# Two pairs of gathered rows per unit on TensorE, through the same two buffers, in units 1 to 7 of a PEER layer

## The chip, the cores and the metric

One core of one Trainium2 chip. The metric is the device time of one execution in microseconds (us); lower is better.

## The reference, cut to what matters

One decoder layer over 256 tokens of width 2048. Its last part is a PEER feed-forward: for each token and each of 8 heads, two searches of the best 16 of 128 keys give 16 experts out of 16,384, and then

```python
u = peer_u[eb]                                   # (256 tokens, 128 chosen rows, 2048)
a = gelu(einsum('td,tkd->tk', xb, u))            # one dot product per token and row
out = einsum('tk,tkd->td', wb * a, peer_v[eb])
```

The change is about the first einsum: 256 x 128 rows of `peer_u` have to be gathered, and each is dotted with its token's `h1`.

## The kernel before, in words

The 128 partitions hold 128 tokens. A **unit** is one head of one half of the tokens: units 0 to 7 are the first half (T = 0), 8 to 15 the second. A unit has 16 rows, k = 0 to 15; row k is one gather (`gather_u`, L1833): one indirect DMA issued by GpSimd (POOL) that fetches, for each of the 128 tokens, one row of 2048 floats, 1 MB in all. POOL issues all gathers in a written order, each behind the wait for its buffer (`wait_free`, L1819).

There are eight buffers of 1 MB. Six form a ring for the rows dotted on VectorE (DVE): the gather of such a row waits until the dot of the row six places earlier is done. Two more hold rows 0 and 1 of a unit, the **pair**. DVE's dot is one instruction (L1633) of 128x2048 with both inputs in SBUF. The pair goes another way (`dots_pair`, L814): in 8 blocks, TensorE (PE) turns two 128-column pieces of both rows into PSUM (L826), ScalarE (ACT) copies the block to `ut` (`pair_copies`, L1204), and PE multiplies it with `h1` turned (`products`, L830). Two buffers each for the PSUM block and `ut` carry it from engine to engine. At the end, `pair_dots` (L1637) on DVE picks the diagonal of the product, two instructions of 128x128 with one input in PSUM. The two buffers of the pair are free as soon as the eighth block is turned (semaphore `ut_turned`), before the products end.

Unit 0 uses DVE only. In units 1 to 15 DVE does 9 dots (k = 2 to 10), the pair's two short instructions, and 5 dots (k = 11 to 15). In units 1 to 13 the steps of the search for the unit after next (`topk`, L1569) stand between them. POOL gathers k = 0 to 15 in order, the pair first; in unit 1 four ring rows come before the pair. After unit 15 the second einsum starts: gathers of `v_rows` for part of the columns, and dense panels of `peer_v` on PE for the others.

Of the kernel before, what the change touches and what calls it, by code (L numbers as in the profile page):

```python
# [33 lines left out]
PH, NKEY, TOPK = 8, 128, 16  # L34
# [32 lines left out]
RING = 8  # L67
HEAD_RING = 4

PAIR = (0, 1)  # L70
PAIR_AFTER = 9
ROW_RING = 6
BLOCKS = KT // 2
PER_UNIT = P // 4 // 8
# [41 lines left out]
def decoder_layer(nc, x, meta_tokens, ln0_g, ln0_b, w_in, b_if, conv_w, mh_norm_w, p_a, p_b, w_o,  # L116
# [5 lines left out]
    with ctx:  # L122
# [155 lines left out]
        def S(name):  # L278
            if name not in sems:
                sems[name] = ctx.enter_context(nc.semaphore(name))  # L280
            return sems[name]
# [23 lines left out]
        u_in = [S(f"u_in{j}") for j in range(RING)]  # L305
# [5 lines left out]
        TOKR = [(0, META), (META, P), (META + P, P)]  # L311
        HCRED, BCRED = SLOT_N, NB

        def dot_place(u, k):

            if u == 0:
                return k + 1
            if k in PAIR:
                return u * TOPK + PAIR_AFTER + k + 1
            return u * TOPK + k - 1 + (2 if k - 2 >= PAIR_AFTER else 0)  # L320

        def row_number(u, k):

            return (u - 1) * (TOPK - 2) + k - 2

        def row_slot(u, k):
            if u == 0:
                return k % HEAD_RING
            return ROW_RING + k if k in PAIR else row_number(u, k) % ROW_RING

        def wait_row(eng, u, k):

            j = row_slot(u, k)
            if u == 0:
                eng.wait_ge(u_in[j], 16 * (k // HEAD_RING + 1))
            elif k in PAIR:
                eng.wait_ge(u_in[j], 16 * u)
            else:
                eng.wait_ge(u_in[j], 16 * ((TOPK // HEAD_RING if j < HEAD_RING else 0) + row_number(u, k) // ROW_RING + 1))

# [13 lines left out]
        def _(sp):  # L354
# [57 lines left out]
            for i in range(NKEY):  # L412
                j = i % RAWS
                if i == 0:
                    sp.wait_ge(S("topk_done"), NT * PH)
                elif i == 1:
                    sp.wait_ge(S("ut_used"), (2 * PH - 1) * BLOCKS)
                elif i == 3:
                    sp.wait_ge(S("dots_done"), 2 * PH * TOPK)
                elif i >= RAWS:  # L420
                    sp.wait_ge(S("panel_done"), i - RAWS + 1)
                set_apart(sp)
                sp.dma_start(v_raw[j][:, :], peer_v[i * P:(i + 1) * P, :]).then_inc(vr_in[j], 16)
                if i == NKEY - 8:

                    sp.wait_ge(S("panel_done"), 64)
                    for t, v in ((g2_bc, ln2_g), (b2_bc, ln2_b)):
                        sp.dma_start(t[:, :], v[0].partition_broadcast(P)).then_inc(S("bc2_in"), 16)
# [8 lines left out]
        def _(pe):  # L437
# [241 lines left out]
            for g in range(3):  # L679
                tokens_group(g + G_WO, mh, ml, 0, g % 2, wo_free(g),  # L680
                             {1: lambda: sum_blocks(3), 6: lambda: residual(0)} if g == 0 else {2: lambda: residual(g)},
                             before=merged_wait if g == 0 else None)
# [128 lines left out]
                    last = mm(ps[:, 3 * T + n, 0:b - a], alpha_i[:, :], h1[:, T, a:b], True, False)  # L811
                last.then_inc(S("tile_opened"), 1)

            def dots_pair(u):  # L814

                T, m = u // PH, u - 1
                o = ps[:, 5 - 3 * (m % 2), 0:256]

                def turn(b):
                    g = m * BLOCKS + b  # L820
                    if g >= 2:
                        pe.wait_ge(S("ut_copied"), g - 1)
                    for n in range(2):
                        for r, k in enumerate(PAIR):
                            kt = 2 * b + n
                            last = nc.tensor.transpose(ps[:, 3 + g % 2, (2 * n + r) * P:(2 * n + r + 1) * P],  # L826
                                                       u_rows[row_slot(u, k)][:, kt * P:(kt + 1) * P], ident[:, :])
                    last.then_inc(S("ut_turned"), 1)

                def products(b):  # L830
                    g = m * BLOCKS + b
                    pe.wait_ge(S("ut_copied"), g + 1)
                    if b == 0 and m >= 2:
                        pe.wait_ge(S("dots_done"), dot_place(u - 2, PAIR[1]))
                    for n in range(2):
                        kt = 2 * b + n
                        last = mm(o, h1t[T][:, kt, :], ut[:, g % 2, n * 256:(n + 1) * 256], kt == 0, kt == KT - 1)
                    last.then_inc(S("ut_used"), 1)

                for k in PAIR:  # L840
                    wait_row(pe, u, k)
                turn(0)
                for b in range(BLOCKS):
                    if b + 1 < BLOCKS:
                        turn(b + 1)
                    products(b)
# [29 lines left out]
            h1_turn(0)  # L876
            h1_turn(1)
            for u in range(1, 2 * PH):
                dots_pair(u)
                if u == PH:  # L880
                    slots_turn(0)
                if u >= PH:
                    for c in range((u - PH) * PER_UNIT, (u - PH + 1) * PER_UNIT):
                        place(c)
# [22 lines left out]
        def _(act):  # L907
# [293 lines left out]
                    A(h1t[T][:, 4 * c:4 * c + 4, :].rearrange("p a t -> p (a t)"), ps[:, bank, :], ACT.Copy  # L1201
                      ).then_inc(S("h1t_copied"), 1)

            def pair_copies(u):  # L1204
                for b in range(BLOCKS):
                    g = (u - 1) * BLOCKS + b
                    act.wait_ge(S("ut_turned"), g + 1)
                    if g >= 2:
                        act.wait_ge(S("ut_used"), g - 1)
                    A(ut[:, g % 2, :], ps[:, 3 + g % 2, :], ACT.Copy).then_inc(S("ut_copied"), 1)  # L1210
# [50 lines left out]
            gelu(0)  # L1261
            softmax_exp(2)
            for u in range(1, 2 * PH):
                pair_copies(u)
                if u > 1:
                    gelu(u - 1)
                if 3 <= u + 1 < 2 * PH:
                    softmax_exp(u + 1)
                if u == PH:
                    slots_copy(0)  # L1270
                    act.wait_ge(S("slots_copied"), 1)
                if u >= PH:
                    for c in range((u - PH) * PER_UNIT, (u - PH + 1) * PER_UNIT):
                        one_hots(c)
                        if c % PER_UNIT:
                            w_copy(c - 1)
                    w_copy(c)
# [10 lines left out]
        def _(dve):  # L1288
# [345 lines left out]
                                       h1[:, u // PH, :], ALU.mult, ALU.mult,  # L1634
                                       accum_out=dots[:, u % 2, k:k + 1]).then_inc(S("dots_done"), 1)

            def pair_dots(u):  # L1637

                m = u - 1
                dve.wait_ge(S("ut_used"), (m + 1) * BLOCKS)  # L1640
                for r, k in enumerate(PAIR):
                    bank = 5 - 3 * (m % 2)
                    dve.wait_ge(S("dots_done"), dot_place(u, k) - 1)
                    V.scalar_tensor_tensor(junk2[:, :], ps[:, bank, r * P:(r + 1) * P], 1.0, ident[:, :], ALU.mult, ALU.mult,
                                           accum_out=dots[:, u % 2, k:k + 1]).then_inc(S("dots_done"), 1)
# [51 lines left out]
            dve.wait_ge(S("sc_copied"), NT * 4)  # L1697
            topk(2, scores_of(2), {6: lambda: coefs(0)})

            def unit_part(u, n):  # L1700

                if n == PAIR_AFTER:
                    pair_dots(u)
                else:
                    dot(u, n + 2 if n < PAIR_AFTER else n + 1)
                if n == 8 and u > 1:
                    coefs(u - 1)
                if n == 8 and u == PH:
                    scale_acc(0)

            for u in range(1, 2 * PH):
                parts = TOPK - 1
                if u + 2 < 2 * PH:
                    topk(u + 2, scores_of(u + 2), {n + 1: lambda n=n: unit_part(u, n) for n in range(parts)})
                else:
                    for n in range(parts):
                        unit_part(u, n)
# [44 lines left out]
        def _(pool):  # L1762
# [56 lines left out]
            def wait_free(u, k):  # L1819

                if u == 0:
                    if k >= HEAD_RING:
                        pool.wait_ge(S("dots_done"), dot_place(0, k - HEAD_RING))
                elif k in PAIR:
                    if u > 1:
                        pool.wait_ge(S("ut_turned"), (u - 1) * BLOCKS)
                elif row_number(u, k) >= ROW_RING:
                    before = row_number(u, k) - ROW_RING
                    pool.wait_ge(S("dots_done"), dot_place(before // (TOPK - 2) + 1, before % (TOPK - 2) + 2))
                elif row_slot(u, k) < HEAD_RING:  # L1830
                    pool.wait_ge(S("dots_done"), dot_place(0, TOPK - HEAD_RING + row_slot(u, k)))

# [23 lines left out]
            for k in range(TOPK):  # L1856
                gather_u(0, k)
            indices(1)
            for k in range(2, 2 + HEAD_RING):
                gather_u(1, k)  # L1860
            pool.wait_ge(S("halves_used"), GROUPS * HALVES + HCRED)
            pool.wait_ge(S("qk_done"), NT * 4)
            for k in PAIR + tuple(range(2 + HEAD_RING, TOPK)):
                gather_u(1, k)
            for u in range(2, 2 * PH):
                indices(u)
                for k in range(TOPK):
                    gather_u(u, k)
            for n in range(NT * SLOTS):
                gather_v(n)  # L1870
# [33 lines left out]
```

## Time and profile before

| | |
|---|---|
| median of 3 runs | 2397.64 us (2397.33 to 2400.06) |
| the profiled execution, its own time | 2398.14 us |
| span of that execution, first to last instruction | 2396.3 us |
| mean granted TensorE clock | 0.904 of full speed |
| gathers of rows of u: first and last of units 1 to 15 | about 1221 us to 1805 us |

The span has three parts: dense projections, bound by PE, to about 1240 us; the dots, to about 1845 us; the second einsum, to the end. POOL's records need care: one lasts from when the engine takes the gather up to when its descriptors are written, and it can be stretched by a wait inside it. The DMA share is that of 16 queues; it passes 1 slightly because packets overlap.

### The profile page before, as it was taken

Reading aid. Unit: us, or ns where it says so; the run is one execution under the profiler, and the core shown is the slowest. Engines: PE = TensorE matmul, PEld = TensorE weight load, DVE = VectorE, ACT = ScalarE, POOL = GpSimd, SP = SyncE. Lnnn points to the kernel's source line nnn. Section 1 sums busy time; section 2 is a strip of 40 time slices with the busy share of each in tenths; the row PEclk is TensorE's granted clock in tenths of the full one; section 3 lists DMA queues with packets and bytes.
Section 4 is the critical chain, followed back from the end, with each engine's and each line's share of the span. In section 5 each row is a group of like instructions: output and inputs, shape, how many; then the busy total and the mean of one; then the engine's idle time right before and its main releaser. Section 6 shows DMA issues by size and latency. Waiting matters only on the chain.

```text
span 2396.3 us, 30725 instructions
## 1 busy us (share of the span) xinstructions
PE 1975.6 (82%) x10800; PEld 1619.9 (68%) x10800; DVE 1603.7 (67%) x2299; ACT 868.5 (36%) x1467; POOL 952.2 (40%) x559
## 2 busy tenths in 40 slices
PE   6999999999999999999972424264645899999996
PEld 5888899998888988887961313253534666666663
DVE  5444455455444555555989999999997866666666
ACT  4444434444444444446431212278685500000000
POOL 0000000000000000000248888888885288878884
PEclk9999999999999999999996756566656999999998
DMA  5444465655655655552989999999998299999997
GB/s 164 127 139 139 141 191 168 200 177 180 194 188 176 202 184 189 189 181 91 366 335 399 420 421 421 409 420 418 411 419 343 106 411 412 411 410 411 411 407 286
DMA packets 217056, 675.01 MB, mean 282 GB/s; under 512 B 18784, under 2 KB 68320, under 8 KB 183520
## 3 DMA queue, kind: packets, MB, share of 16 engines
q0 software_dynamic: 57488, 393.25, 40.3%
q1 hardware_dynamic: 159456, 280.32, 35.3%
q8 instruction: 64, 1.05, 0.2%
q14 instruction: 48, 0.39, 0.0%
HBM read 671.42 MB, written 2.10 MB: 281 GB/s over the span
## 4 chain that ended last, share of the span: by engine, by line
PE 47%; issue 22%; POOL 10%; DMA 10%; DVE 9%; ACT 2%; DVEq 0%; POOLq 0%; ACTq 0%; SPq 0%
PE ps L439 46%; DMA u_rows<-in_peer_u,idx_all 8%; POOL v_rows L1851 7%; POOL u_rows L1838 3%; DMA v_rows<-in_v_gathered,idx_all 2%; DVE junk L1633 2%; DVE ohs L1666 1%; ACT hi L911 0%; DVE ohs L1663 0%; DVE h L1681 0%; PE ps L524 0%; DVE st L1328 0%; DVE ki L1593 0%; DVE pos L1606 0%; DVE pos L1603 0%
## 5 line engine op out<-in xcount | busy, mean ns | idle before, releaser
L1296 DVE TENSOR_TENSOR lo<-raw,hi 128x1024 fp32r<-128x1024 f32 x368 | 448.6, 1225 | 489.5 <-ACT hi L911 488.9
L1838 POOL DMA_INDIRECT u_rows<-in_peer_u,idx_all x256 | 537.5, 2100 | 170.9 <-issue 73.6
L911 ACT ACTIVATE hi<-raw 128x1024 fp32r<-128x1024 f32 x376 | 397.3, 1059 | 568.2 <-PE ps L439 561.5
L1633 DVE SCALAR_TENSOR_TENSOR junk<-u_rows,h 128x2048 bf16<-128x2048 f32 x226 | 514.7, 2280 | 31.9 <-DMA u_rows<-in_peer_u,idx_all 31.9
L439 PE MATMUL ps<-v_raw,wt 128*128 128x368 f32 x1536 | 475.4, 472 | 2.8 <-DMA v_raw<-in_peer_v 2.0
L1851 POOL DMA_INDIRECT v_rows<-in_v_gathered,idx_all x256 | 391.8, 1530 | 147.4 <-issue 79.6
L439 PE MATMUL ps<-xh,hi 128*128 128x256 f32 (+2 forms) x1536 | 440.6, 287 | 2.4 <-ACT qkv L911 1.3
L439 PE MATMUL ps<-xh,lo 128*128 128x256 f32 (+2 forms) x1536 | 435.6, 284 | 0.0
L439 PE MATMUL ps<-xl,hi 128*128 128x256 f32 (+2 forms) x1536 | 435.0, 283 | 0.0
L1681 DVE SCALAR_TENSOR_TENSOR h<-v_rows,coef_all,h 128x944 f32<-128x944 f32 x256 | 307.6, 1202 | 173.4 <-DMA v_rows<-in_v_gathered,idx_all 172.2
L439 PEld LDWEIGHTS ps<-v_raw,wt 128*128 128x128 f32 x1536 | 291.7, 190 | 186.2 <-DMA v_raw<-in_peer_v 2.6
L1784 POOL TENSOR_TENSOR rstd<-rstd,m_half 128x1 f32<-128x1 f32 (+1 forms) x7 | 5.8, 823 | 820.1 <-DVE rstd L1537 800.4
L439 PEld LDWEIGHTS ps<-xh,hi 128*128 128x128 f32 x1536 | 290.4, 189 | 12.2 <-issue 8.5
L439 PEld LDWEIGHTS ps<-xl,hi 128*128 128x128 f32 x1536 | 290.9, 189 | 0.0
L439 PEld LDWEIGHTS ps<-xh,lo 128*128 128x128 f32 x1536 | 290.2, 189 | 0.0
L826 PE MATMUL ps<-ident,u_rows 128*128 128x128 f32 x480 | 87.2, 321 | 208.3 <-issue 196.5
L826 PEld LDWEIGHTS ps<-ident,u_rows 128*128 128x128 f32 x480 | 73.2, 170 | 223.7 <-issue 214.7
L439 PE MATMUL ps<-ohs 128*128 128x128 f32 x512 | 102.1, 363 | 136.8 <-ACT ohs L911 126.2
L439 PEld LDWEIGHTS ps<-ohs 128*128 128x128 f32 x512 | 87.8, 259 | 152.2 <-ACT ohs L911 136.4
L911 ACT ACTIVATE ut<-ps 128x512 f32<-128x512 f32 x120 | 71.6, 597 | 291.8 <-PE ps L826 291.8
L439 PE MATMUL ps<-ut,h1t 128*128 128x256 f32 x480 | 140.1, 424 | 0.1
L439 PE MATMUL ps<-hi,xh 128*128 128x512 f32 x256 | 101.8, 398 | 1.8 <-DVE t_y L1452 1.3
(227 smaller groups left out, 2497.1 us busy)
## 6 DMA issues: line engine op xcount, KB each, us to landing
raw<-in_w_in SPq DMA_DIRECT2D x96, 1024.0 KB, 5.4
v_raw<-in_peer_v SPq DMA_DIRECT2D x128, 552.0 KB, 7.8
raw<-in_w_in SPq DMA_DIRECT2D x64, 256.0 KB, 3.2
raw<-in_w_in SPq DMA_DIRECT2D x32, 512.0 KB, 4.6
raw<-in_p_a SPq DMA_DIRECT2D x16, 1024.0 KB, 5.0
raw<-in_p_b SPq DMA_DIRECT2D x16, 1024.0 KB, 5.0
raw<-in_w_o SPq DMA_DIRECT2D x16, 1024.0 KB, 5.0
raw<-in_peer_wq SPq DMA_DIRECT2D x16, 1024.0 KB, 6.8
```

The source lines that it names most:

```text
L439: return nc.tensor.matmul(o, a, b, start=start, stop=stop)
L826: last = nc.tensor.transpose(ps[:, 3 + g % 2, (2 * n + r) * P:(2 * n + r + 1) * P], u_rows[row_slot(u, k)][:, kt * P:(kt + 1) * P], ident[ ...
L911: return nc.scalar.activation(o, i, f, **kw)
L1296: V.tensor_tensor(raw_lo[:, hh // 2, k4, :] if kept else lo[:, hh % SLOT_N, :, :], raw[:, hh // 2, k4, :], (kept_hi(hh) if kept else hi[:, ...
L1633: V.scalar_tensor_tensor(junk[:, n % 2, :], u_rows[row_slot(u, k)][:, :], 1.0, h1[:, u // PH, :], ALU.mult, ALU.mult, accum_out=dots[:, u ...
L1666: ins = V.tensor_scalar(o[:, 0, q, :], iota[:, :], slots_t[:, 1, t0 + q:t0 + q + 1], slots_t[:, 0, t0 + q:t0 + q + 1], ALU.is_equal, ALU.mult)
L1681: V.scalar_tensor_tensor(h1[:, T, FD:D], v_rows[n % VRING][:, :], coef_all[:, T, s:s + 1], h1[:, T, FD:D], ALU.mult, ALU.add).then_inc(S(" ...
L1784: Q.tensor_tensor(rstd[:cnt, n:n + 1], rstd[:cnt, n:n + 1], m_half[:cnt, 0:1], ALU.pow).then_inc(S(name + "_rstd"), 1)
L1838: Q.indirect_dma_start(u_rows[slot][:, :], None, peer_u, bass.IndirectOffsetOnAxis(ap=idx_all[:, n:n + 1], axis=0)).then_inc(u_in[slot], 16)
L1851: Q.indirect_dma_start(v_rows[n % VRING][:, :], None, v_gathered, bass.IndirectOffsetOnAxis(ap=idx_all[:, n:n + 1], axis=0)).then_inc(v_in ...
```

## The change

Units 1 to 7 send two pairs through PE, rows 0 and 1 and rows 2 and 3; units 8 to 15 keep one pair. Both pairs of a unit use the same two buffers, so the second pair's gathers wait until the first pair has been turned, and the next unit's first pair until the second has. POOL's order in units 2 to 7 becomes: first pair, 6 ring rows, second pair, 6 ring rows. In unit 1: ring rows 4 to 7, first pair, rows 8 and 9, second pair, rows 10 to 15. DVE's order becomes: 9 dots, first pair's two short instructions, 3 dots, second pair's two. The sizes of all buffers stay.

```diff
-PAIR = (0, 1)
-PAIR_AFTER = 9
+PAIRS = (0,) + (2,) * (PH - 1) + (1,) * PH
+PAIR_AFTER = (9, 14)
+SECOND_GATHERED = 6
...
+        def dot_order(u):
+
+            rows, order = vector_rows(u), []
+            for n in range(TOPK):
+                for q in range(PAIRS[u]):
+                    if len(order) == PAIR_AFTER[q] and pair_rows(q)[0] not in order:
+                        order += pair_rows(q)
+                if rows:
+                    order.append(rows[0])
+                    rows = rows[1:]
+            for q in range(PAIRS[u]):
+                if pair_rows(q)[0] not in order:
+                    order += pair_rows(q)
+            return tuple(order)
...
+        def gather_order(u):
+
             if u == 0:
-                return k + 1
...
+                return tuple(range(TOPK))
+            rows = vector_rows(u)
+            order = pair_rows(0) + rows
+            if PAIRS[u] == 2:
+                order = pair_rows(0) + rows[:SECOND_GATHERED] + pair_rows(1) + rows[SECOND_GATHERED:]
+            return order
...
         def row_slot(u, k):
             if u == 0:
                 return k % HEAD_RING
-            return ROW_RING + k if k in PAIR else row_number(u, k) % ROW_RING
+            return ROW_RING + k % 2 if k < 2 * PAIRS[u] else row_number(u, k) % ROW_RING
...
             for u in range(1, 2 * PH):
-                dots_pair(u)
+                for q in range(PAIRS[u]):
+                    dots_pair(u, q)
...
             for u in range(1, 2 * PH):
-                pair_copies(u)
+                pair_copies(u, 0)
                 if u > 1:
                     gelu(u - 1)
                 if 3 <= u + 1 < 2 * PH:
                     softmax_exp(u + 1)
+                if PAIRS[u] == 2:
+                    pair_copies(u, 1)
...
-                elif k in PAIR:
-                    if u > 1:
-                        pool.wait_ge(S("ut_turned"), (u - 1) * BLOCKS)
+                elif k < 2 * PAIRS[u]:
+                    if pair_number(u, k // 2):
+                        pool.wait_ge(S("ut_turned"), pair_number(u, k // 2) * BLOCKS)
...
-            for k in PAIR + tuple(range(2 + HEAD_RING, TOPK)):
-                gather_u(1, k)
+            for k in gather_order(1):
+                if k not in vector_rows(1)[:HEAD_RING]:
+                    gather_u(1, k)
             for u in range(2, 2 * PH):
                 indices(u)
-                for k in range(TOPK):
+                for k in gather_order(u):
                     gather_u(u, k)
```

`vector_rows(u)` are the rows from 2 x PAIRS[u] to 15, `pair_number(u, q)` counts the pairs through PE, and the numbers that the semaphores are waited for follow the new orders.

## Rows read from the trace of the kernel before

**Rows 1.** The page: busy time by engine, and DMA over 40 slices of 59.9 us.

```profile
PE 1975.6 (82%) x10800; PEld 1619.9 (68%) x10800; DVE 1603.7 (67%) x2299; ACT 868.5 (36%) x1467; POOL 952.2 (40%) x559
...
DMA  5444465655655655552989999999998299999997
GB/s 164 127 139 139 141 191 168 200 177 180 194 188 176 202 184 189 189 181 91 366 335 399 420 421 421 409 420 418 411 419 343 106 411 412 411 410 411 411 407 286
```

**Rows 2.** Stretches: start:end, length, busy PE PEld DVE ACT POOL, clock, DMA share, GB/s.

```profile
1343.00:1424.00 81.00, 25.84 (x128) 21.45 (x128) 78.58 (x143) 15.92 (x26) 71.22 (x33) 0.65 1.01 421
1248.00:1250.00 2.00, 2.00 (x14) 1.72 (x13) 2.00 (x7) 1.10 (x2) 1.70 (x2) 1.00 0.55 147
```

**Rows 3.** Timeline of DVE in unit 14 (no search steps): two dots in succession.

```profile
1781.41 2.29 DVE L1633 SCALAR_TENSOR_TENSOR junk<-u_rows,h 128x2048 bf16<-128x2048 f32 x1 [0.19 <-DMA u_rows<-in_peer_u,idx_all]
...
1783.89 2.29 DVE L1633 SCALAR_TENSOR_TENSOR junk<-u_rows,h 128x2048 bf16<-128x2048 f32 x1 [0.18 <-DMA u_rows<-in_peer_u,idx_all]
```

**Rows 4.** Timeline of PE: a pair's first and last turned blocks, units 1, 2 and 8.

```profile
1242.43 1.94 PE L826 MATMUL ps<-ident,u_rows 128*128 128x128 f32 x8 [11.75 <-DMA u_rows<-in_peer_u,idx_all]
...
1252.48 0.60 PE L826 MATMUL ps<-ident,u_rows 128*128 128x128 f32 x4
...
1275.51 1.94 PE L826 MATMUL ps<-ident,u_rows 128*128 128x128 f32 x8 [20.61 <-issue]
...
1286.08 0.60 PE L826 MATMUL ps<-ident,u_rows 128*128 128x128 f32 x4
...
1519.78 1.94 PE L826 MATMUL ps<-ident,u_rows 128*128 128x128 f32 x8 [27.07 <-issue]
...
1531.08 0.60 PE L826 MATMUL ps<-ident,u_rows 128*128 128x128 f32 x4
```

**Rows 5.** Timeline of POOL: the gathers that matter in units 1 and 2.

```profile
1234.14 0.94 POOL L1838 DMA_INDIRECT u_rows<-in_peer_u,idx_all  x1 [0.30 <-issue]
1243.03 0.93 POOL L1838 DMA_INDIRECT u_rows<-in_peer_u,idx_all  x1 [7.95 <-DVE junk L1633]
...
1265.23 2.75 POOL L1838 DMA_INDIRECT u_rows<-in_peer_u,idx_all  x1 [0.30 <-DVE junk L1644]
1268.28 2.58 POOL L1838 DMA_INDIRECT u_rows<-in_peer_u,idx_all  x1 [0.30 <-issue]
1271.17 2.58 POOL L1838 DMA_INDIRECT u_rows<-in_peer_u,idx_all  x1 [0.30 <-issue]
```

**Rows 6.** Timeline of DVE in units 1 and 2: dots beside those gathers.

```profile
1239.94 2.27 DVE L1633 SCALAR_TENSOR_TENSOR junk<-u_rows,h 128x2048 bf16<-128x2048 f32 x1
...
1253.69 2.27 DVE L1633 SCALAR_TENSOR_TENSOR junk<-u_rows,h 128x2048 bf16<-128x2048 f32 x1
...
1267.77 2.28 DVE L1633 SCALAR_TENSOR_TENSOR junk<-u_rows,h 128x2048 bf16<-128x2048 f32 x1
1269.98 0.08 DVE L1633 DVE_READ_ACCUMULATOR junk<-u_rows,h 128x1 f32 x1
```

**Rows 7.** The gathers started from 1214 to 1215 us, to an idle queue: record and landing.

```profile
L1838 POOL DMA_INDIRECT u_rows<-in_peer_u,idx_all x1: 1137/1137/1137, 1214.8 to 1214.8; - x1
...
DMA to landing us min/median/max: 5.6/5.6/5.6
```

**Rows 8.** The gathers started from 1204 to 1206 us, beside a dot: record and landing.

```profile
L1838 POOL DMA_INDIRECT u_rows<-in_peer_u,idx_all x1: 2954/2954/2954, 1205.0 to 1205.0; - x1
...
DMA to landing us min/median/max: 7.5/7.5/7.5
```

**Rows 9.** Stretches around one pair's turning in unit 5 (columns as in rows 2).

```profile
1396.00:1398.00 2.00, 0.09 (x1) 0.12 (x2) 2.00 (x4) 0.00 (x0) 1.72 (x1) 0.50 1.02 426
...
1404.00:1406.00 2.00, 2.00 (x13) 1.77 (x13) 2.00 (x3) 1.16 (x2) 2.00 (x1) 1.00 1.01 422
...
1410.00:1412.00 2.00, 1.13 (x5) 0.67 (x4) 2.00 (x5) 1.97 (x3) 2.00 (x1) 1.00 1.03 430
...
1414.00:1416.00 2.00, 0.00 (x0) 0.00 (x0) 2.00 (x2) 0.00 (x0) 1.69 (x2) 0.50 1.02 426
```

More of the change, by code:

```diff
@@ L312, in decoder_layer, with vector_rows, pair_rows, pair_number @@
         HCRED, BCRED = SLOT_N, NB
+        def vector_rows(u):
+            return tuple(range(2 * PAIRS[u], TOPK))
+        def pair_rows(q):
+            return (2 * q, 2 * q + 1)
+        def pair_number(u, q):
+            return sum(PAIRS[:u]) + q
+        def dot_order(u):
[11 more added lines that the diff above has]
+            return tuple(order)
         def dot_place(u, k):
+            return u * TOPK + dot_order(u).index(k) + 1
+        def gather_order(u):
             if u == 0:
-                return k + 1
-            if k in PAIR:
-                return u * TOPK + PAIR_AFTER + k + 1
-            return u * TOPK + k - 1 + (2 if k - 2 >= PAIR_AFTER else 0)
-        def row_number(u, k):
-            return (u - 1) * (TOPK - 2) + k - 2
+                return tuple(range(TOPK))
[4 more added lines that the diff above has]
+            return order
+        def row_number(u, k):
+            return sum(len(vector_rows(w)) for w in range(1, u)) + k - 2 * PAIRS[u]
+        def row_of_number(n):
+            u = 1
+            while n >= len(vector_rows(u)):
+                n, u = n - len(vector_rows(u)), u + 1
+            return u, vector_rows(u)[n]
         def row_slot(u, k):
@@ L335, in wait_row @@
                 eng.wait_ge(u_in[j], 16 * (k // HEAD_RING + 1))
-            elif k in PAIR:
-                eng.wait_ge(u_in[j], 16 * u)
+            elif k < 2 * PAIRS[u]:
+                eng.wait_ge(u_in[j], 16 * (pair_number(u, k // 2) + 1))
             else:
@@ L416, in _ @@
                 elif i == 1:
-                    sp.wait_ge(S("ut_used"), (2 * PH - 1) * BLOCKS)
+                    sp.wait_ge(S("ut_used"), sum(PAIRS) * BLOCKS)
                 elif i == 3:
@@ L812, in tile_open, with dots_pair @@
                 last.then_inc(S("tile_opened"), 1)
-            def dots_pair(u):
-                T, m = u // PH, u - 1
+            def dots_pair(u, q):
+                T, m = u // PH, pair_number(u, q)
                 o = ps[:, 5 - 3 * (m % 2), 0:256]
@@ L823, in turn @@
                     for n in range(2):
-                        for r, k in enumerate(PAIR):
+                        for r, k in enumerate(pair_rows(q)):
                             kt = 2 * b + n
@@ L833, in products @@
                     if b == 0 and m >= 2:
-                        pe.wait_ge(S("dots_done"), dot_place(u - 2, PAIR[1]))
+                        w, z = next((w, z) for w in range(2 * PH) for z in range(PAIRS[w]) if pair_number(w, z) == m - 2)
+                        pe.wait_ge(S("dots_done"), dot_place(w, pair_rows(z)[1]))
                     for n in range(2):
@@ L838, in products @@
                     last.then_inc(S("ut_used"), 1)
-                for k in PAIR:
+                for k in pair_rows(q):
                     wait_row(pe, u, k)
@@ L1202, in h1_copy, with pair_copies @@
                       ).then_inc(S("h1t_copied"), 1)
-            def pair_copies(u):
+            def pair_copies(u, q):
                 for b in range(BLOCKS):
-                    g = (u - 1) * BLOCKS + b
+                    g = pair_number(u, q) * BLOCKS + b
                     act.wait_ge(S("ut_turned"), g + 1)
@@ L1635, in dot, with pair_dots @@
                                        accum_out=dots[:, u % 2, k:k + 1]).then_inc(S("dots_done"), 1)
-            def pair_dots(u):
-                m = u - 1
+            def pair_dots(u, q):
+                m = pair_number(u, q)
                 dve.wait_ge(S("ut_used"), (m + 1) * BLOCKS)
-                for r, k in enumerate(PAIR):
+                for r, k in enumerate(pair_rows(q)):
                     bank = 5 - 3 * (m % 2)
@@ L1698, in _, with unit_steps @@
             topk(2, scores_of(2), {6: lambda: coefs(0)})
+            def unit_steps(u):
+                order = dot_order(u)
+                return [k for k in order if k >= 2 * PAIRS[u] or k % 2 == 0]
             def unit_part(u, n):
-                if n == PAIR_AFTER:
-                    pair_dots(u)
+                k = unit_steps(u)[n]
+                if k < 2 * PAIRS[u]:
+                    pair_dots(u, k // 2)
                 else:
-                    dot(u, n + 2 if n < PAIR_AFTER else n + 1)
+                    dot(u, k)
                 if n == 8 and u > 1:
@@ L1711, in _ @@
             for u in range(1, 2 * PH):
-                parts = TOPK - 1
+                parts = len(unit_steps(u))
                 if u + 2 < 2 * PH:
@@ L1823, in wait_free @@
                         pool.wait_ge(S("dots_done"), dot_place(0, k - HEAD_RING))
-                elif k in PAIR:
-                    if u > 1:
-                        pool.wait_ge(S("ut_turned"), (u - 1) * BLOCKS)
+                elif k < 2 * PAIRS[u]:
+                    if pair_number(u, k // 2):
+                        pool.wait_ge(S("ut_turned"), pair_number(u, k // 2) * BLOCKS)
                 elif row_number(u, k) >= ROW_RING:
-                    before = row_number(u, k) - ROW_RING
-                    pool.wait_ge(S("dots_done"), dot_place(before // (TOPK - 2) + 1, before % (TOPK - 2) + 2))
+                    pool.wait_ge(S("dots_done"), dot_place(*row_of_number(row_number(u, k) - ROW_RING)))
                 elif row_slot(u, k) < HEAD_RING:
@@ L1858, in _ @@
             indices(1)
-            for k in range(2, 2 + HEAD_RING):
+            for k in vector_rows(1)[:HEAD_RING]:
                 gather_u(1, k)
```

## The prediction, made before the change was built

> **What bounds the kernel now.** I read the page first, to find the stretch that the change touches: from about 1260 us the DMA row stands at 9 and the rate at 399 to 421 GB/s until the dots end [rows 1]. Then the windows: over 81 us of it DVE is busy for 78.6, so it is nearly full as well, beside a DMA share of 1.01 at 421 GB/s [rows 2]. Which of the two sets the pace they can't say. The timeline of unit 14 settles it: there are no search steps, DVE waits before each dot for a row to land, and dots follow each other at 1783.89 - 1781.41 = 2.48 us [rows 3]. A row of 1.0486 MB in 2.49 us is 421 GB/s, the rate of the middle units as well. So sixteen rows cost at least 16 x 2.49 = 39.8 us of transfer. The real pace comes from PE's first turn in units 2 and 8: (1519.78 - 1275.51) / 6 = 40.71 us per unit [rows 4]. DVE's load can therefore be worth 0.9 us per unit at most, whatever is taken from it. What keeps the queue full is that eight buffers are refilled early; that is what the change touches.
>
> **What the change removes.** In units 1 to 7, two dots of 2.28 us go from DVE and two short instructions of about 0.3 us (an estimate from their size: a sixteenth of the columns of a dot [rows 6], plus start-up) come. That is about 4 us of DVE's 40.7, but only 0.9 of them can show, as above.
>
> **What it adds: a loop.** The two pair buffers are now filled and turned twice per unit. Each filling waits for the previous turning; each turning waits for both rows. The loop has four terms, and twice its length is the least time of a unit.
>
> 1. Turned to POOL's gather. No row shows POOL released by PE. DVE's first dot of unit 1 ends at 1242.21 and POOL's gather, idle till then, starts at 1243.03 [rows 5, 6]: 0.8 us, which I take. Bounds: 0 and 1.1.
> 2. First gather's start to second row's landing. To an idle queue and beside no dot, one gather takes 5.6 us to land [rows 7]; a second row adds a transfer, so 5.6 + 2.49 = 8.1 us. Beside a dot it is longer. In unit 2, nothing is left to wait for by either gather of the pair, since the turning ended at 1252.48 + 0.60 = 1253.08 [rows 4]. Yet the gather of 1268.28 lasts 2.58 us, to 1270.86, 0.8 us after the dot of 1267.77 has ended (1270.06 with its read); at 1234.14, when DVE has no dot, one lasts 0.94 [rows 5, 6]. The same shows in landing: 7.5 us for a gather that lasted 2.95 against 5.6 for one of 1.14 [rows 7, 8]. So POOL gets a gather out only between dots. Unit 2's pair took from 1265.23 to PE's start at 1275.51, 10.3 us, with both gathers held. Bounds: 8.1 and 10.3.
> 3. Landing to PE's start, about 0.1 us.
> 4. Turning, first block's start to last block's end: 10.65, 11.17 and 11.90 us in units 1, 2 and 8 [rows 4]. I take 11.3. Bounds: 10.65 and 11.9.
>
> "SBUF — State Buffer" in the Trainium skill, section "Who interferes with whom", says that a VectorE instruction with two inputs in SBUF contends with a GpSimd instruction that reads SBUF, and that the later one waits for the whole of the earlier. By that rule a pair's gathers are held by dots and not by `pair_dots`, whose one input is in PSUM; the trace agrees (2.58 us against 0.94). Without the rule term 2 would be 8.1 and the loop 20.3 us, and the total about +10 us; with it the loop is about 21.5 and the total about +24.
>
> Term 2 in the steady state, with the first gather of a pair at time 0. The six ring rows ahead of it land one per 2.49 us, beginning that long after the pair ahead; the loop is 12.2 us plus term 2, so they land at -9.7, -7.2, -4.7, -2.2, +0.3 and +2.8, whatever term 2 is. DVE, with a dot of 2.3 and about 0.5 of search steps per row, has them nearly as they come. At a unit's end: a dot from -1.3 to 1.0 holds the first gather until 1.8; the second starts at 2.1, is held by the dot from 1.75 to 4.05 until 4.9, and lands 4.7 us after it is out (5.6 less 0.94) at 9.6. Amid the unit the dots stand a little earlier and the same steps give about 9.0. So the loops are 21.8 and 21.2 us, 21.5 in the mean. The DMA needs 8 x 2.49 = 19.9 us for the eight rows of a loop and so is idle for 1.6 us of each.
>
> **The sum.**
>
> - Units 2 to 7, from the first pair of unit 2 to that of unit 8: 12 loops x 21.5 = 258.0 us, against 244.3 now [rows 4]: +13.7.
> - Unit 1. Now POOL issues its last gather without a dot's release at 1234.14 and the next at 1243.03, when the first dot has freed a buffer [rows 5]. After the change the one after row 9 is the second pair's first, which waits for the turning: 1253.08 + 0.8 = 1253.9. The dot of 1253.69 holds it until 1256.8, so it lands at 61.5, the second row at 64.0. Turned at 1275.4; the next pair's gathers start at 1276.2 and land 9.2 us on, at 1285.4; PE starts at 1285.5 where it now starts at 1275.5: +10.0. The queue runs dry from about 1247 to 1259, where it now shows one dip, to 0.55 in 2 us [rows 2].
> - Unit 8 on: order and buffers are as now, and the stretch behind is bound by the DMA too [rows 1], so the delay stays whole: 0. I give nothing back; at most the 0.9 us a unit of above.
> - PE has 2 x 13 us of pair work in 43 us, ACT 16 copies of 0.6: free, they are idle beside it. The second pair is behind `gelu` and `softmax_exp` on ACT, which wait for dots of the unit before; those are done some 8 us after the first pair's gathers, before the first pair is turned. DVE waits for each pair's products later than they come. Both cost 0; if that cover were gone, each would lengthen the loop one for one.
>
> Sum: 10.0 + 13.7 = +23.7 us. Against the profiled execution's own time, 2398.14 + 23.7 = 2421.8; the median of the runs stands 0.5 us lower, so 2421.3 us, +1.0%.
>
> **Rivals.**
>
> *The loop is hidden.* If DVE, waiting for rows more often, leaves gaps in which POOL's gathers go out at once, term 2 is 8.1 to 8.5 and the loop 20.3: the unit's pace is that of now and only unit 1 pays. Time: 2397.6 + 10 = 2408. For it: DVE has 4 us fewer to do. Against: at the time of a pair's gathers, rows 5 and 6 of the loop are just landing, so a dot nearly always runs. 0.17.
>
> *The loop is longer.* Term 2 at 10.3 and term 4 at 11.9 give 23.1 us: 12 x 23.1 - 244.3 = +33, with unit 1 +44, that is 2442. Worse if TensorE's clock does not rise: the pair of unit 5, after some 27 us without work, starts at 0.50, which is 1.2 GHz, has 1.00 some 6 us later, and is back at 0.50 by 1414, some 3 us after its last work [rows 4, 9]. With two pairs the pause is 21.5 - 13 = 8 us, still longer than those 3, so I expect the same start at 1.2 GHz; the spread of term 4, 10.65 to 11.9 us, is as much as I let the clock move. 0.14.
>
> *Faster.* DVE sets the pace and the transfers can go quicker: then 4 us of DVE's work come off each of seven units, -28, less unit 1's 10: 2380. It decides from the point where the queue moves a row in under 2.49 us, and where the loop is under 20.3. For it: DVE's 78.6 of 81 us. Against: share 1.01, and 2.48 us per row in unit 14 where DVE waits. If only the 0.9 us a unit comes, -5.4 + 10 is still slower. 0.04.
>
> *The change does less than it says*: the second pair could wait for the ring instead of the first pair. It can't: the wait on `ut_turned` is in the program order of POOL.
>
> **How the numbers follow.** Forecast (loops of 21 to 22.4 us, +18 to +35): 0.62; hidden 0.17; longer 0.14; faster 0.04; the rest, a mix near no change, 0.03. The predicted time is the forecast's, 2421. The range runs from 2406 (loops at 20.2) to 2436 (loops at 22.7) and leaves out 2 in 10. A measurement of this kernel tells some 0.2%, 4.8 us, from no change. Faster by more: 0.04. Within it: 0.05. Slower by more: 0.91.
>
> **What would show it.** In the profile after: POOL idle before the second pair's first gather of unit 1, from about 1235 to 1254 us, and the DMA share near 0 for some 10 us behind; in units 2 to 7, POOL idle before each pair's first gather and released by PE; PE's pairs starting every 21.5 us; windows with a DMA share of 0.9 to 0.95; DVE at some 35 of 43 us (39.5 less 4), waiting for rows of u. Wrong would be: a DMA share of 1.01 through units 2 to 7 (hidden); pairs 23 us apart or more (longer); POOL's gathers of a pair 0.94 us long beside dots, which takes away term 2's working; a DVE wait on `ut_used` or an ACT wait inside a loop, which I cost at nothing; and a rate above 421 GB/s.

## The result and the profile after

Slower: 2433.15 us in the median (2430.78 to 2434.02, 4 runs) against 2398.51 us for the kernel before, run beside it; ratio 1.0141, 95% interval 1.0128 to 1.0154. That is +34.6 us. The profiled execution took 2432.44 us with a span of 2430.6, against 2398.14 and 2396.3.

The page after, the lines that answer to [rows 1]:

```profile
DMA  5444465565556555544979999999999299999996
GB/s 161 132 142 141 139 191 178 169 196 184 190 190 191 180 186 189 190 156 152 367 291 383 383 381 375 402 410 421 418 400 390 80 412 411 412 410 411 411 410 274
```

The digits of the DMA row still stand at 9 behind unit 1, and only the rate tells that something is missing: 375 to 383 GB/s over units 2 to 7, where [rows 1] has 399 to 421. So the windows are read next, columns as in [rows 2]. The first is where the queue ran dry in unit 1, the second the steady state:

```profile
1246.00:1256.00 10.00, 9.41 (x54) 7.75 (x53) 10.00 (x15) 3.58 (x6) 1.59 (x1) 0.98 0.02 7
...
1400.00:1480.00 80.00, 48.94 (x241) 40.53 (x240) 67.41 (x137) 24.28 (x40) 46.15 (x28) 0.80 0.96 383
```

For ten microseconds of unit 1 next to nothing was moved (share 0.02, 7 GB/s), while DVE worked off what had landed. In the steady state the share is 0.96, and DVE is busy for 67.4 of 80 us. POOL's timeline shows what the queue waited for. These are its gathers around unit 1; [rows 5] has the same stretch before:

```profile
1234.42 0.94 POOL L1888 DMA_INDIRECT u_rows<-in_peer_u,idx_all  x1 [0.30 <-issue]
1254.41 2.59 POOL L1888 DMA_INDIRECT u_rows<-in_peer_u,idx_all  x1 [19.05 <-PE ps L867]
1257.31 0.94 POOL L1888 DMA_INDIRECT u_rows<-in_peer_u,idx_all  x1 [0.30 <-issue]
...
1277.72 1.97 POOL L1888 DMA_INDIRECT u_rows<-in_peer_u,idx_all  x1 [12.02 <-PE ps L867]
```

POOL sat for 19.05 us until PE had turned the first pair (L867 is the turning). It had ring rows left to ask for, behind the pair in its order, and free buffers for them from about 1243 on, when the kernel before asked for its next one [rows 5]. The same wait comes back at every pair. POOL's waits from 1290 to 1530 us (total, times, longest):

```profile
POOL u_rows L1888 <- PE ps L867: 69.6, 11, 7.3
```

The kernel before has no such row. PE's timeline, the first blocks turned of the first three pairs and of unit 8's, as in [rows 4]:

```profile
1242.97 1.94 PE L867 MATMUL ps<-ident,u_rows 128*128 128x128 f32 x8 [12.07 <-DMA u_rows<-in_peer_u,idx_all]
...
1265.72 1.94 PE L867 MATMUL ps<-ident,u_rows 128*128 128x128 f32 x8 [10.31 <-issue]
...
1286.92 1.94 PE L867 MATMUL ps<-ident,u_rows 128*128 128x128 f32 x8 [8.20 <-issue]
...
1551.48 1.94 PE L867 MATMUL ps<-ident,u_rows 128*128 128x128 f32 x8 [9.77 <-issue]
```

This places the loss. Unit 2's first pair is 1286.92 - 1275.51 = 11.4 us late, of which 0.5 were there at unit 1's first pair already (1242.97 against 1242.43), as a difference between two executions. From there to unit 8's are 12 loops, 264.56 us or 22.05 each, where six units took 244.27: 20.3 more. From unit 8 to the end the span adds 34.3 - 31.7 = 2.6. That is scatter as far as the traces tell: this stretch lasts 876.5 us before and 879.1 after, and 876.1 to 881.7 in the eleven runs below, whatever their change.

### The profile page after: what moved, and what is told of

The parts are those of the page before. It is cut to its first block, busy times and chain, and to the rows that moved or that the text cites. A ratio compares the mean times of both kernels' runs of the same rounds, so it can differ in the third digit from the quotient of the medians.

```text
span 2430.6 us, 31740 instructions
## 1 busy us (share of the span) xinstructions
PE 2067.2 (85%) x11248; PEld 1696.8 (70%) x11248; DVE 1578.3 (65%) x2299; ACT 902.0 (37%) x1523; POOL 886.0 (36%) x559
## 4 chain that ended last, share of the span: by engine, by line
PE 71%; DMA 11%; issue 9%; DVE 7%; ACT 1%; POOL 1%; DVEq 0%; POOLq 0%; ACTq 0%; SPq 0%
PE ps L480 67%; DMA u_rows<-in_peer_u,idx_all 10%; PE ps L867 3%; DVE junk L1678 1%; POOL u_rows L1888 1%; DVE ohs L1711 1%; DMA v_raw<-in_peer_v 1%; ACT hi L954 1%; DVE ohs L1708 0%; PE ps L565 0%; DVE st L1373 0%; ACT tok L954 0%; PE ps L635 0%; PE ps L613 0%; DVE y L1804 0%
## 5 line engine op out<-in xcount | busy, mean ns | idle before, releaser
L1888 POOL DMA_INDIRECT u_rows<-in_peer_u,idx_all x256 | 471.4, 1841 | 270.4 <-PE ps L867 107.0
L1678 DVE SCALAR_TENSOR_TENSOR junk<-u_rows,h 128x2048 bf16<-128x2048 f32 x212 | 483.3, 2282 | 90.0 <-DMA u_rows<-in_peer_u,idx_all 89.9
L1901 POOL DMA_INDIRECT v_rows<-in_v_gathered,idx_all x256 | 391.7, 1530 | 145.9 <-issue 80.7
L867 PE MATMUL ps<-ident,u_rows 128*128 128x128 f32 x704 | 127.5, 321 | 151.5 <-issue 139.4
L867 PEld LDWEIGHTS ps<-ident,u_rows 128*128 128x128 f32 x704 | 106.9, 169 | 175.2 <-issue 161.7
L954 ACT ACTIVATE ut<-ps 128x512 f32<-128x512 f32 x176 | 105.0, 597 | 292.2 <-PE ps L867 292.2
L480 PE MATMUL ps<-ut,h1t 128*128 128x256 f32 x704 | 205.4, 424 | 0.2 <-ACT ut L954 0.2
L480 PEld LDWEIGHTS ps<-ut,h1t 128*128 128x128 f32 x704 | 134.5, 213 | 23.0 <-ACT ut L954 10.3
```

The source lines that it names most:

```text
L480: return nc.tensor.matmul(o, a, b, start=start, stop=stop)
L954: return nc.scalar.activation(o, i, f, **kw)
L1678: V.scalar_tensor_tensor(junk[:, n % 2, :], u_rows[row_slot(u, k)][:, :], 1.0, h1[:, u // PH, :], ALU.mult, ALU.mult, accum_out=dots[:, u ...
L1888: Q.indirect_dma_start(u_rows[slot][:, :], None, peer_u, bass.IndirectOffsetOnAxis(ap=idx_all[:, n:n + 1], axis=0)).then_inc(u_in[slot], 16)
L1901: Q.indirect_dma_start(v_rows[n % VRING][:, :], None, v_gathered, bass.IndirectOffsetOnAxis(ap=idx_all[:, n:n + 1], axis=0)).then_inc(v_in ...
```

## The experiments

Each was run beside the kernel before, whose median there was 2398.6 to 2399.1 us.

**Where the loss sits: unit 1 alone, and all but unit 1.**

```diff
-PAIRS = (0,) + (2,) * (PH - 1) + (1,) * PH
+PAIRS = (0, 2) + (1,) * (2 * PH - 2)              # unit 1 only
+PAIRS = (0, 1) + (2,) * (PH - 2) + (1,) * PH      # all but unit 1
```

> Two pairs in unit 1 alone, one pair in units 2 to 15. Loop theory: only the queue that runs dry in unit 1 is left, where the first pair of unit 2 came 11.4 us later in the changed kernel: +10 to +12 us over the kernel before, about 2409. Rival, that the loss is spread evenly over the units with two pairs (a seventh of 34.6 us each): +5 us, about 2403.

> Two pairs in units 2 to 7, one in unit 1. Loop theory: 12 loops of 22.0 us where six units took 244.3 us: +20 us, and what is left of unit 1 is nothing: +19 to +23 us over the kernel before, about 2419. Rival, that unit 1's loss only moves to the first unit with two pairs: the full +34.

Unit 1 only: 2409.91 us, ratio 1.0044 (1.0029 to 1.0059), +10.9. All but unit 1: 2421.17 us, 1.0089 (1.0074 to 1.0105), +22.1. The two make 33.0 of 34.6 us. Both rivals fall: each of units 2 to 7 with two pairs costs some 3.5 us by its loops, and unit 1 costs three times that through the pause in which nothing is asked for.

**The loop taken away: two buffers more.**

```diff
-            return ROW_RING + k % 2 if k < 2 * PAIRS[u] else row_number(u, k) % ROW_RING
+            return ROW_RING + k if k < 2 * PAIRS[u] else row_number(u, k) % ROW_RING
...
-                    if pair_number(u, k // 2):
-                        pool.wait_ge(S("ut_turned"), pair_number(u, k // 2) * BLOCKS)
+                    if u > 1:
+                        pool.wait_ge(S("ut_turned"), (pair_number(u - 1, k // 2) + 1) * BLOCKS)
```

The two buffers lie where the dense part kept its weights, free in units 1 to 7. (The lines that make the ring ten buffers long and count their semaphores are left out here.)

> The changed kernel with two buffers more, so that the second pair has its own and waits for the turning of the second pair of the unit before, not for the first pair of its own. DVE's, ACT's and PE's orders and POOL's order of gathers stay. Loop theory: no loop of two fillings and two turnings is left, the queue stays full, units 1 to 7 go at 39.8 to 40.7 us: no loss, or up to 7 us less than the kernel before, 2391 to 2399, DMA share 1.01. Rival, that the second pair's work or its place in the orders of PE, ACT and DVE costs the time: it stays at 2420 or more.

2395.63 us, ratio 0.9988 (0.9979 to 0.9997), and once more 2395.80 us, 0.9988 (0.9979 to 0.9997), expected as

> The run with own buffers once more, on the same chip as the kernel with ten buffers and one pair: 3.4 us faster than the kernel before, 2 to 5.

So the whole loss is gone, and it is 3.4 us faster than the kernel before (3.3 the second time). The work of two pairs on PE, ACT and DVE and its place in their orders is all still there. Its window in the steady state, and PE's first blocks of the first pairs of units 2 and 8:

```profile
1400.00:1480.00 80.00, 52.23 (x253) 43.38 (x252) 68.85 (x143) 25.48 (x42) 60.09 (x33) 0.76 1.01 421
```

```profile
1273.55 1.94 PE L868 MATMUL ps<-ident,u_rows 128*128 128x128 f32 x8 [6.26 <-issue]
...
1517.83 1.94 PE L868 MATMUL ps<-ident,u_rows 128*128 128x128 f32 x8 [7.00 <-issue]
```

The share is back at 1.01 and 421 GB/s, a unit takes (1517.83 - 1273.55) / 6 = 40.71 us, exactly the 40.71 of the kernel before, and DVE, with its two dots fewer, is idle for 11 of 80 us. So DVE's relief shows nothing here, because the DMA is the bound. (This traced execution took 2401.32 us, the slowest of its eleven; in the trace of the second run, 2395.58 us, share and rate are the same and a unit takes 40.55 us.)

**A known dose in the loop.**

```diff
-                        pool.wait_ge(S("ut_turned"), pair_number(u, k // 2) * BLOCKS)
+                        pool.wait_ge(S("ut_used"), pair_number(u, k // 2) * BLOCKS)
```

> The changed kernel, but each filling of the pair buffers waits until the pair's products are used, not until its last block is turned: some 1.8 us later by the trace of the kernel before. A dose of known size in the loop. Loop theory: 14 releases x 1.8 us = +25 us over the changed kernel, about 2458. If the loop is hidden in most of its rounds (then the loss is elsewhere), less than +8 us.

2450.02 us (2441.71 to 2453.15), ratio 1.0201 (1.0183 to 1.0219): +16.9 on the changed kernel in the medians, +20.0 in the profiled spans, less than the 25 expected. The four runs lie 11 us apart, so the loops in the profile say more than the total. PE's first blocks of units 2 and 8:

```profile
1287.34 1.94 PE L867 MATMUL ps<-ident,u_rows 128*128 128x128 f32 x8 [8.98 <-issue]
...
1573.20 1.94 PE L867 MATMUL ps<-ident,u_rows 128*128 128x128 f32 x8 [11.35 <-issue]
```

POOL's gather now starts 2.63 us after the last turned block, where it was 0.81: a dose of 1.82. The 12 loops take 285.86 us, 1.78 more each: the dose in full. Up to unit 2 it cost only 0.4 us: the first gather of unit 1's second pair came 1.7 us later (1256.11), but no dot held it, and PE started 8.5 us behind it instead of 11.3.

**The loop made shorter than its eight rows' transfer.**

```diff
-BLOCKS = KT // 2
+BLOCKS = KT // 4
```

> The changed kernel with 4 blocks per pair instead of 8 (the columns from 1024 on of the dot products of all pairs are left out): a turning takes about 6.3 us instead of 11.4. The loop falls to about 17 us, under the 19.9 that the DMA needs for its eight rows. Loop theory: units 2 to 7 lose nothing any more, and unit 1 some 6 us instead of 11: 2398 to 2408. Rival, that the extra work on PE and ACT or the new orders cost the time in proportion to their work: half of 34.6 stays, 2416.

2402.37 us, ratio 1.0013 (1.0003 to 1.0023), +3.3. Its windows of unit 1 and of the steady state:

```profile
1246.00:1256.00 10.00, 3.96 (x21) 3.08 (x19) 10.00 (x15) 1.19 (x2) 6.44 (x3) 0.84 0.37 126
1290.00:1530.00 240.00, 94.35 (x384) 75.23 (x384) 208.26 (x423) 45.48 (x74) 163.20 (x96) 0.67 1.01 419
```

The steady state loses nothing (1.01), with the same two buffers filled twice per unit: from unit 2's first pair to unit 8's it is 243.1 us, against 244.3 before, although POOL still waits for PE at the pairs (47.1 us in 11 waits). What remains is unit 1, 37.6 us from its first pair to unit 2's against 33.1. So the shared buffers cost time with a loop of 22.05 us and none with one that would be about 17 by its terms; that the change lies at the 19.9 us of eight rows fits both, but no run stands near it.

**Does slack elsewhere in the queue make a loop good?**

```diff
+PAIRS = (0,) + (1, 2, 1, 2, 1, 2, 1) + (1,) * PH
```

> Shared pair buffers, two pairs in units 2, 4 and 6 only. If each pair behind another costs its own 2.1 us (a loop of 22.0 us against the 19.9 us of its eight rows), whatever comes later: 3 units x 2 loops x 2.1 = +12 to +13 us over the kernel before, about 2411. Rival, that only the mean distance of pairs counts (27 us here, above 22) and the queue makes good what it lost: within 3 us of the kernel before.

2410.99 us, ratio 1.0051 (1.0036 to 1.0066), +11.9: the local count, six loops of 2 us. Units with one pair give nothing back, since their own transfers have no slack.

**What holds a gather: shorter dots.**

```diff
+                w = D // 2 if 1 <= u < PH else D           # 64 in the second of these runs
-                V.scalar_tensor_tensor(junk[:, n % 2, :], u_rows[row_slot(u, k)][:, :], 1.0,
+                V.scalar_tensor_tensor(junk[:, n % 2, 0:w], u_rows[row_slot(u, k)][:, 0:w], 1.0,
```

> The changed kernel with DVE's dots of units 1 to 7 over the first 1024 of the 2048 columns (half of these dot products is left out), so each takes 1.2 us instead of 2.3. If dots hold POOL's gathers (term 2), a pair's two rows are held less: 8.7 to 9.2 us to landing instead of 9.8, 12 loops give back 8 to 13 us: 2420 to 2425. Rival, that term 2 is long because of the DMA queue alone: no change, 2433.

2431.71 us, ratio 1.0144 (1.0127 to 1.0161): no gain, a miss for my term 2. Over its 12 loops a pair took 10.1 us from first gather to PE's start (9.8 in the changed kernel), though half of the pairs' gathers went out in 0.94 us and none took over 1.94 (2.87 in the changed kernel). I formed a second theory, that the queue itself is slow when it starts again, and took the dots away nearly altogether:

> The changed kernel with DVE's dots of units 1 to 7 over the first 64 of the 2048 columns (almost all of these dot products is left out), so that no dot can hold a gather for more than a fraction of a microsecond. The run with half dots gained nothing, yet in the run with the later release a pair whose first gather was held for some 2.9 us landed 10.2 to 10.7 us after its start and one held for less than 1.5 us landed after 8.7 to 9.2. If holding is what makes term 2 of the loop 9.8 us in the mean, it falls to 8.2 to 8.6 here and 12 loops give back 14 to 19 us: 2414 to 2420. Rival, that the queue itself is slow when it starts again (second row of a pair 3.8 to 4.1 us behind the first, held or not): term 2 stays at 9.4 to 10.2, the time at 2428 to 2436.

2425.33 us, ratio 1.0118 (1.0101 to 1.0134), -7.8 on the changed kernel. The time is outside both forecasts; a pair took 9.6 us in the mean over the 12 loops, as the second theory said. The 12 loops give back 4.9 us, half by those 0.2 us and half by turnings that were 0.2 us shorter, and unit 1 gives back 1.7. One pair of this run, POOL's two gathers and PE's start:

```profile
1360.86 0.94 POOL L1889 DMA_INDIRECT u_rows<-in_peer_u,idx_all  x1 [11.15 <-PE ps L867]
1362.10 0.94 POOL L1889 DMA_INDIRECT u_rows<-in_peer_u,idx_all  x1 [0.30 <-issue]
```

```profile
1371.47 1.94 PE L867 MATMUL ps<-ident,u_rows 128*128 128x128 f32 x8 [9.61 <-issue]
```

and the windows between them:

```profile
1363.00:1364.00 1.00, 0.00 (x0) 0.00 (x0) 0.07 (x1) 0.00 (x0) 0.69 (x2) 1.00 0.55 213
1364.00:1371.00 7.00, 0.00 (x0) 0.00 (x0) 1.99 (x11) 0.00 (x0) 4.97 (x6) 0.69 0.98 377
```

Neither gather is held, and the pair still needs 10.6 us. From 1364 to 1371 the queues move 7 x 377 GB/s = 2.64 MB, and the pair is 2.10: part of the ring rows asked for right behind has been fetched before the pair's second row is whole. And they do it at 377, not 421.

These windows also say how much each of the two is worth. With the 0.21 MB of the first window, 2.10 MB had been moved by about 1369.0, 8.1 us after the first gather; PE started only 2.5 us later, and rows from behind were moved meanwhile. Counted in the same way over the 12 loops, from windows of 0.5 us, the queues have moved all that was asked for up to and with the pair 7.7 us after its first gather, and PE starts at 9.6, when some 0.7 MB of later rows have been moved as well (in the changed kernel 8.1 and 9.8). So the larger part is not that the queues were slow, but that they moved rows from behind before the pair was whole. That is read from traces; no run holds back the rows behind a pair.

**What DVE's two dots are worth, and a deeper queue.** Half dots in the kernel before; and the kernel before with the two buffers added to the ring in units 1 to 7.

> The kernel before with the same half dots in units 1 to 7 (half of these dot products is left out): DVE loses 14 x 1.1 us per unit, four times what the change takes from it. If the DMA sets the pace (16 x 2.49 us a unit), at most 7 units x 0.9 = 6 us are gained: 2392 to 2397. Rival, that DVE sets it: several times 7 x 4 us, 2370 or less.

> The kernel before with the two buffers of the run with own buffers added to the ring in units 1 to 7 (eight ring buffers, one pair): more rows asked for ahead, DVE's work as before. If what the run with own buffers gained (3.4 us) comes from DVE's two dots fewer, this one gains nothing, within 1 us of the kernel before. Rival, that it comes from the deeper queue: 2 to 4 us faster.

Half dots: 2394.81 us, ratio 0.9982 (0.9972 to 0.9992), -4.2, with 15 us of DVE's work gone per unit: the DMA sets the pace. Ten buffers: 2397.45 us, 0.9992 (0.9983 to 1.0001), -1.6, between the two forecasts. The totals don't divide the 3.4 us of the run with own buffers; PE's timelines, one trace each, say where they lie:

| us, from PE's first turned block | unit 1 to unit 2 | unit 2 to unit 8 |
|---|---|---|
| kernel before | 33.1 | 244.3 |
| own buffers, first and second run | 29.7 and 30.9 | 244.3 and 243.3 |
| ten buffers, one pair | 29.9 | 246.0 |
| half dots in the kernel before | 29.8 | 242.9 |

In unit 1, 2 to 3 us are gained (33.1 to 34.9 us in the three traces with eight buffers, whole dots and one pair there), and with ten buffers they come without any relief of DVE. The dip of [rows 2], a share of 0.55 from 1248 to 1250 us, stands at 0.99 to 1.03 in all four. In units 2 to 7 DVE's two dots fewer are worth 0 to 1 us in all; why the ten buffers took 1.8 us longer there is open.

## Why the prediction was right, point by point

The measured 2433.15 us lie in the range of 2406 to 2436, but near its end: 11.9 us above the 2421.3 of the sum. The mechanism was right, and one term of the sum was too small.

- *The DMA is the bound, DVE's relief is worth 0.9 us a unit at most.* Shown: four times the relief gives 4.2 us in all, of which 1.4 lie in units 2 to 7 by the trace, 0.2 a unit. What else makes a unit 40.7 us and not 39.8 is open.
- *A loop of two fillings and two turnings sets the unit's pace.* Shown from three sides: gone with own buffers, gone with a short turning (and the eight buffers as they were), longer by the dose. POOL's release by PE and the pairs' distance are in the profile.
- *Unit 1, +10.0.* 11.4 in the profile, 10.9 without the 0.5 that were there before it; +10.9 alone. The steps came true to a microsecond: the second pair's first gather at 1254.4 (forecast 1253.9), held by the dot to 1257.0 (1256.8). The miss is the pair's second row: 1257.31 + 8.3 = 1265.6, where I had 1264.0.
- *Units 2 to 7, +13.7.* 20.3. The step that failed is the size of term 2 of the loop, and with the second row of unit 1's pair it is most of the 11 us by which the total was short. Of 22.05 us, the terms measured 12.24 from PE's start to POOL's next gather (I had 12.1) and 9.81 from there to PE's start (9.3 and 0.1). The 12 loops of 22.05 instead of 21.5 us make the 6.6 us that the sum lacked here, 4.9 of them by term 2 and 1.7 by the turnings.
- *Term 2's working.* Its lower bound, 8.1 us, added one transfer at the full rate of 2.49 us to a lone gather's 5.6. As a bound it stood: no pair that PE released took less, and the nearest took 8.13 and 8.17. As what a pair takes that nothing holds, it was too low. (In the working for the steady state, 4.7 us from a gather's going out to its landing should be 5.6 - 1.14 = 4.5, since the lone gather lasted 1.14 [rows 7].) The landings after the pause of unit 1, first gather alone and both:

```profile
DMA to landing us min/median/max: 7.1/7.1/7.1
...
DMA to landing us min/median/max: 7.1/7.7/8.3
```

  The first row landed at 1254.41 + 7.1 = 1261.5, the second at 1265.6, 4.1 us later. Holding by dots is real in POOL's records, and in the run with the later release the pairs held for 2.8 us or more landed after 10.2 to 10.7 us, those held under 1.5 after 8.7 to 9.2. But with almost no holding left the mean fell only from 9.81 to 9.60: what the gathers gain by going out at once, the rows behind them gain too, and those are then moved before the pair is whole. So the 9.4 was nearer to the measured 9.8 than its reason deserves, which was luck: it was built as 8.1 plus holding, and without holding a pair takes 9.6. The queues' slow first windows are no reason, for the lone gather's 5.6 us have them in it: 115 and 238 GB/s from 1216 to 1218. The rule of the Trainium skill that I weighed ("SBUF — State Buffer", "Who interferes with whom") describes the records well: 0.94 us when no dot runs, up to 2.87 beside one; the total that I drew from it, +24 with it and +10 without, does not hold: without holding it is still +27.
- *The loop is hidden* (0.17) failed for just that reason: it needed 8.1 to 8.5 us, and in the changed kernel the shortest of the 12 pairs took 8.7; only single pairs of the runs with later release and tiny dots came under 8.5. *Longer* (0.14) was half true: single pairs took 10.2 to 10.8 us. The clock had no part beyond what was forecast: PE started a pair at 0.50 (1418 to 1422) and had 1.00 by 1424, and the turnings of 10.6 to 12.0 us are about as long as before.
- *Unit 8 on, 0.* The profile shows 2.6 us, no more than the scatter of that stretch. (The last gather of rows of u is at 1828 us in the kernel before, not at about 1805 as the table there has it; nothing in the sum hangs on it.)
- *No wait on `gelu`, on `ut_used` or in DVE.* Right: POOL's waits name PE's turning, ACT waited for PE's turning and DVE for rows of u alone, and with own buffers nothing else came up.

## What to carry to other kernels

A buffer filled and emptied twice per round is a loop of its own: issue, queue, landing, use, release. Add up its terms from the trace and compare them with what the queue moves in that time; here 22.05 us stood against 19.9, and it cost 2.1 us per loop although DVE, the busiest engine of this stretch, had become less busy. In an in-order queue such a wait also stops all that stands behind it, dearest where the round begins (11 us in unit 1). Price the landing of a pair by a measured landing of two rows with others asked for right behind them, not by a lone one plus the spacing in a full stream.

## What the runs showed of the hardware that was not expected

- A DMA queue that has run short can start slowly. In the changed kernel two windows right behind a dip (share 0.49 from 1413 to 1414) are busy but move little:

```profile
1414.00:1415.00 1.00, 0.00 (x0) 0.00 (x0) 1.00 (x2) 0.00 (x0) 0.70 (x2) 0.50 1.03 270
1415.00:1416.00 1.00, 0.00 (x0) 0.00 (x0) 1.00 (x1) 0.00 (x0) 1.00 (x1) 0.50 0.98 254
```

  A share of 1 is therefore no sign of the full rate; 254 to 270 GB/s stand here against 421. It isn't so behind every dip: the run with tiny dots moves 401 GB/s in the first window behind its own (1364 to 1365). What makes the packets slow was not tested.
- A gather can be whole later than its turn: 2.64 MB were moved while the 2.10 MB of a pair landed, and over 12 loops a pair was whole 1.9 us later in the mean than the bytes up to it had been moved (7.7 and 9.6 us). A part of that is what any gather takes from its last byte to its landing. That the 16 queues run apart would explain it; that is argued, not shown.
